# Triangular inverse of a gated delta rule: one full-array product with a crossed matrix in place of two quarter products

## The reference

```python
m = jnp.where(strict, jnp.einsum('nbhid,nbhjd->nbhij', kb, kc) * decay, 0.0)
t_inv = lax.linalg.triangular_solve(eye + m, jnp.broadcast_to(eye, m.shape), left_side=True, lower=True)
u = t_inv @ (vc * bc[..., None])
w = t_inv @ (kb * jnp.exp(gcum)[..., None])
qk = jnp.einsum('nbhid,nbhjd->nbhij', qc, kc) * decay
```

## Time and profile before

| | us |
|---|---|
| median of 3 runs | 2912.72 |
| lowest and highest of them | 2904.73, 2915.39 |
| the profiled execution | 2918.56 |
| its span on the core | 2916.8 |

### The profile page before, as it was taken

The page is one execution under the profiler, slowest core; times in us unless marked ns, Lnnn a source line. Parts: engine busy times, 40 slices in busy tenths (PEclk is TensorE's granted clock), DMA queues, the critical chain, the costliest instruction groups (busy, mean ns, idle before and its releaser), DMA issues.

```text
span 2916.8 us, 62045 instructions
## 1 busy us (share of the span) xinstructions
PE 2791.2 (96%) x24636; PEld 2709.8 (93%) x24636; DVE 2292.1 (79%) x3726; ACT 1491.2 (51%) x2527; POOL 477.1 (16%) x515
## 2 busy tenths in 40 slices
PE   5999989999999998999999999999999999999998
PEld 5999878999999998789999998899987999999998
DVE  7999766669978786666798888789877789777654
ACT  3435555554454475554545446644776544544632
POOL 0016012030110210202103011201036201102202
PEclk9999999999999999999999999999999999999999
DMA  8995403458968752135687894489421489676353
GB/s 341 349 361 204 145 17 123 141 171 327 356 221 288 246 179 82 63 113 188 249 337 260 301 327 171 147 321 344 163 95 66 159 291 345 225 270 238 130 182 136
DMA packets 173162, 632.28 MB, mean 217 GB/s; under 512 B 19216, under 2 KB 19600, under 8 KB 172560
## 3 DMA queue, kind: packets, MB, share of 16 engines
q1 hardware_dynamic: 124128, 450.82, 43.4%
q10 hardware_dynamic: 48816, 178.41, 17.3%
HBM read 628.10 MB, written 1.05 MB: 216 GB/s over the span
## 4 chain that ended last, share of the span: by engine, by line
PE 83%; DVE 10%; ACT 4%; issue 2%; DMA 1%; POOL 0%; ACTq 0%; DVEq 0%; SPq 0%
PE psum L603 24%; PE psum L605 24%; PE psum L604 24%; DVE w_lo L573 3%; DVE qkv L1433 1%; ACT w_hi L561 1%; DVE xl L2713 1%; DMA raw<-stream_dram 1%; PE psum L2811 1%; PE psum L1811 1%; PE psum L2831 1%; PE psum L2825 1%; PE psum L619 1%; ACT sm L2307 1%; PE psum L1821 0%
## 5 line engine op out<-in xcount | busy, mean ns | idle before, releaser
L603 PE MATMUL psum<-h_hi,w_hi 128*128 128x256 f32 (+1 forms) x4464 | 1268.1, 284 | 2.8 <-DVE w_lo L573 1.5
L604 PE MATMUL psum<-h_hi,w_lo 128*128 128x256 f32 (+1 forms) x4464 | 1261.2, 283 | 0.0
L605 PE MATMUL psum<-h_lo,w_hi 128*128 128x256 f32 (+1 forms) x4464 | 1259.3, 282 | 0.0
L573 DVE TENSOR_TENSOR w_lo<-raw,w_hi 128x1024 fp32r<-128x1024 f32 x852 | 1072.9, 1263 | 169.7 <-ACT w_hi L561 168.8
L561 ACT ACTIVATE w_hi<-raw 128x1024 fp32r<-128x1024 f32 x852 | 876.0, 1055 | 360.3 <-DMA raw<-stream_dram 173.2
L603 PEld LDWEIGHTS psum<-h_hi,w_hi 128*128 128x128 f32 x4464 | 850.4, 190 | 11.2 <-DVE w_lo L573 3.8
L605 PEld LDWEIGHTS psum<-h_lo,w_hi 128*128 128x128 f32 x4464 | 848.3, 190 | 0.0
L604 PEld LDWEIGHTS psum<-h_hi,w_lo 128*128 128x128 f32 x4464 | 847.4, 190 | 0.8 <-issue 0.7
L603 PE MATMUL psum<-u_hi,w_hi 128*128 128x256 f32 x1584 | 441.7, 279 | 1.3 <-ACT length L1146 1.3
L605 PE MATMUL psum<-u_lo,w_hi 128*128 128x256 f32 x1584 | 441.5, 279 | 0.0
L604 PE MATMUL psum<-u_hi,w_lo 128*128 128x256 f32 x1584 | 441.5, 279 | 0.0
(11 more groups left out here) (454 smaller groups left out, 3490.0 us busy)
## 6 DMA issues: line engine op xcount, KB each, us to landing
raw<-stream_dram SPq DMA_DIRECT2D x852, 512.0 KB, 4.1
ada_w<-ada_dram ACTq DMA_DIRECT2D x328, 512.0 KB, 5.1
tmp<-c_dram ACTq DMA_DIRECT2D x8, 512.0 KB, 4.2
x<-x_dram SPq DMA_DIRECT2D x1, 1024.0 KB, 10.0
ctx_x<-ctx_dram ACTq DMA_DIRECT2D x1, 1024.0 KB, 4.8
means<-means_dram ACTq DMA_DIRECT2D x1, 1024.0 KB, 4.8
out_dram<-tmp SPq DMA_DIRECT2D x4, 256.0 KB, 2.5
const<-const_dram SPq DMA_DIRECT2D x1, 785.0 KB, 13.5
```

The costliest lines, as they stand in the source:

```text
L573: p.nc.vector.tensor_tensor(p.w_lo[:, slot].rearrange("p k m -> p (k m)"), p.raw[:, slot], p.w_hi[:, slot].rearrange("p k m -> p (k m)").b ...
L603: mm(out, p.w_hi[:, slot, k], hi, start=start, stop=False, skip_group_check=skip)
L604: mm(out, p.w_lo[:, slot, k], hi, start=False, stop=False, skip_group_check=skip)
L605: return mm(out, p.w_hi[:, slot, k], lo, start=False, stop=stop, skip_group_check=skip)
```

## The change

Both blocks of 64 of a head and half are put into one matrix of 128x128, each in the corner off the diagonal ("crossed"), with zeros in the other two corners. One product with this matrix as the stationary operand does what two quarter products did: the upper block's result comes out in the lower partitions and the lower block's in the upper ones. Line 1811's products become half as many, each of 128 rows by 128 columns against 64 moving columns.

GpSimd makes the crossed matrix, into `decay`, by two operations per head: it copies `a_t`'s columns of block `e` to the columns of block `1 - e`, times a constant `half_e` that is one in block `e`'s partitions and zero in the others. It waits for VectorE to have written `a_t` and for ScalarE to have read `decay`. A new semaphore, `masked`, tells TensorE; only level 0 waits for it.

```diff
@@ gdn_gpsimd, for every head h
         v.tensor_tensor(p.qkv[:, h, P:T], p.qkv[:, h, P:T], p.exp_row[:, h % GROUP], ALU.mult).then_inc(p.sem["sq_done"], 1)
+        i = h % GROUP
+        pool.wait_ge(p.sem["pairs_used"], a("pairs_used") + 2 * h + 2)
+        pool.wait_ge(p.sem["turned_used"], a("turned_used") + h + 1)
+        crossed, a_t = (t.rearrange("p (c f n) -> p c f n", c=2, f=2) for t in (p.decay[:, i], p.a_t[:, i]))
+        for e in range(2):
+            ins = v.tensor_scalar(crossed[:, :, 1 - e], a_t[:, :, e], p.c(f"half_{e}"), None, ALU.mult)
+        ins.then_inc(p.sem["masked"], 1)
@@ gdn_tensor, inverse(gq), for every level and head i
                 if level:
                     pe.wait_ge(p.sem["inv_grown"], at("inv_grown", GROWN) + PAIRS + (level - 1) * GROUP + i + 1)
+                if not level:
+                    pe.wait_ge(p.sem["masked"], a("masked") + gq * GROUP + i + 1)
                 for c in range(2):
-                    for e in range(2):
-                        at_c = c * P + e * HALF
-                        ins = mm(p.psum[halves[1 - e], i, c * HALF : c * HALF + HALF],
-                                 p.a_t[halves[e], i, at_c : at_c + HALF], p.inv_h[halves[e], i, 1, c], start=True, stop=True)
+                    ins = mm(p.psum[:, i, c * HALF : c * HALF + HALF], p.decay[:, i, c * P : c * P + P],
+                             p.inv_h[:, i, 1, c], start=True, stop=True)
                 ins.then_inc(p.sem["lp_done"], 1)
```

More of the change, by code:

```diff
@@ L313, in signals @@
         n = dict(gdn_step=2 * PAIRS, cols_ready=1, exp_cum=1, rows_done=8,
-                 kb_ready=8, exponent_ready=16, row_exp=8, decay_ready=8, pairs_done=8, pairs_used=16, sq_done=8,
+                 kb_ready=8, exponent_ready=16, row_exp=8, decay_ready=8, pairs_done=8, pairs_used=16, sq_done=8, masked=8,
                  inv_grown=2 * GROWN, turned_done=8, turned_used=8, first_turned=2 * GROUP, conv_pad=1,
```

## The result

The changed kernel takes 2964.02 us (median; 2958.36 to 2973.33) against 2914.05 us of the kernel before: a ratio of 1.0163 with a 95% interval of 1.0144 to 1.0183. A second set of four executions gave 1.0169 (1.0135 to 1.0203). The profiled execution has a span of 2960.3 us in place of 2916.8, 43.5 more.

The account below looks back on a forecast made before the run. TensorE, busy 96% of the span, was taken to bound the kernel; 60.0 + 3.3 + 1.2 - 55.1 = 9.4 us more gave 2922.1 us against the median, 0.3% slower. The range ran from a little below 2909 to past 2931.5.

Parts of the forecast that it names:

- What stays. The granted clock.: Second and fourth inverse windows: the clock's fall to 1.2 GHz stays as before, costing 1.6 us each, 3.3 us together.
- Rival 3: Levels of the inverse: denser TensorE work keeps the clock up, leaving the kernel 4.5 us slower, 2917; chance 0.14.
- The price of the product: Full products in each level: 16 records at 0.110 us, paced by the weight load, 1.76 us in place of 0.94.
- the forms: Each level: switching the array from 64x64 to 128x128 and back costs 0.30 us, bounds 0.1 and 0.5.
- The stalls: Four inverse windows: all 11.3 us of "issue" waits go, as the new level needs fewer instructions per microsecond.
- Rival 1: Inverse windows: stalls are a price per instruction block, 9.4 us stay, kernel 18.8 us slower, 2931.5; chance 0.14.
- rival 2: Levels: the weight load hides behind the products, kernel 3.8 us faster, 2909; chance 0.10.
- GpSimd: Crossed matrices: 0.49 us per operation, 1.44 us per head, ready 0.4 us before TensorE needs the fourth head's.
- Rival 4: Crossed matrices: GpSimd's operations take twice as long as assumed, 7 to 11 us more, 2929 to 2933; chance 0.10.
- VectorE's slowing: First groups, ahead of the levels: busy GpSimd slows L1549 by 0.3 us and two earlier operations by 0.3; 1.2 us for both layers.
- The sum without the clock: Four inverse windows: the forecast's terms without the clock loss, 60.0 us of levels plus 1.2 for VectorE, less 55.1 before.

Follow-up runs that it names:

- the narrow train: Kernel before, TensorE idle 11.7 us, then 64 unread full-array products of 64 moving columns in the first layer (128 in the second): the 64-column train took 27.54 us.
- the kernel with the filled gap: Changed kernel plus two (second group: four) unread 256-column products where TensorE waits for VectorE ahead of the levels: 2919.11 us, 1.0021.

## Why the prediction was wrong

**The step that failed** is "What stays. The granted clock." It took two falls at 3.3 us together over from the kernel before and kept their number and their length. Neither held. The falls became three and, in the second profile, four, in the first groups too, where there had been none ahead of the merge; and each lasts 27 to 34 us where it lasted 3.4. The gap that a fall needs was there before the change, and filling it removes the fall. It is not a wait for scores, as the prediction reads it: TensorE is idle until VectorE's first steps of the inverse are done (line 1549, 1.97 us in the second groups before, 1.70 after; 0.80 and 1.08 in the first), and the change does touch it. But the length of a fall depends on the work that runs in it, which is shown, and whether it comes seems to depend on the work behind the gap, which is not. The changed levels at full clock sum to 62.17 us, and at the clock they got to 94.77: 32.6 us in the windows in place of 3.3. With the rest of the 43.5, what lies outside the windows, it is up to 36.5. Nothing else in the sum was off by more than a few microseconds. The row that should have raised doubt was the earlier trace rows: it shows a fall under work of another form, and no row showed one under narrow full products. The cost was unknown and ought to have been bounded: a clock that stays down from level 0 to the merge can at most double the 3.00 us of a level, 20 x 3.00 = 60 us more, and a rival with that price should have stood beside the others.

**Rival 3** asked about the clock too, and only in the other direction: it took denser work to be better for it. TensorE did become denser, 24.80 of 24.80 us in place of 10.4 of 14.3, and the clock stayed down all the same. The Trainium skill, "TensorE: Matmul & The Clock Gate", section "What's actually happening", has the half clock as the default that activity releases, by how busy the engine has been. By that rule, with busy read as the profile's busy time, a TensorE without gaps should have been released early in each inverse. The trace doesn't agree for the narrow product: busy for the whole of 27.54 us in the narrow train, it stayed at 1.2 GHz.

**The price of the product** was right. 16 records at 0.110 were forecast; 2.00 us from the first start to the last end, less the last one's 0.275, over 15 steps, is 0.115. The level at full clock takes 3.02 us for the forecast 3.00. What is left for the other products and the forms is 3.02 - 16 x 0.115 = 1.18, for 0.94 + 0.30. That the load sets the pace was right as well: with twice the columns moving, a level takes 3.07 us.

**The stalls** are gone as forecast: "issue" has at most 0.5% of each of the four windows, where it had 15 to 27. Rival 1, a price per block, and rival 2, a hidden load at 2.3 us a level, fall with these two.

**GpSimd** was mis-sized by a little. A crossing operation takes 0.60 us where 0.49 was assumed, and a head's turn 1.75 us (L1652 starts at 374.49 and at 376.24) in place of 1.44, so the fourth matrix was ready 0.57 us late in place of 0.4 us early:

```profile
L1658 POOL TENSOR_SCALAR decay<-a_t,const x32: 598/604/834, 371.4 to 1209.1; 128x128 f32<-128x128 f32 x32
...
374.49 0.45 POOL L1652 TENSOR_TENSOR qkv<-qkv,exp_row 128x128 f32<-128x128 f32 x1
...
376.24 0.45 POOL L1652 TENSOR_TENSOR qkv<-qkv,exp_row 128x128 f32<-128x128 f32 x1
...
378.00 1.08 PE L1818 MATMUL psum<-tmp,decay 128*128 128x64 f32 x4 [0.57 <-POOL decay L1658]
```

TensorE waits 0.57 us there. In the kernel with the filled gap it waits 0.56 in both first groups, and level 0 has 3.76 in place of 3.02 us in them. Rival 4 had the mechanism, at 7 to 11 us; it came to 2 x 0.74 = 1.5. VectorE's slowing was smaller than allowed: the gap ahead of the turns is 1.08 us where it was 0.80, 0.28 instead of 0.6 per layer. Together GpSimd costs 1.5 + 0.6 = 2.1 us for the forecast 1.2.

**The sum without the clock** would have been right to within 2 us: 62.17 - 55.12 + 0.6 = 7.7 us, where the same terms of the forecast give 60.0 + 1.2 - 55.1 = 6.1, and the filled kernel is measured at 1.0021 (1.0007 to 1.0035), that is 2 to 10 us more than before.

Still open: what decides whether a given gap brings the fall (one inverse of the changed kernel had it in one execution and not in the other), how far the narrow products behind the gap bring it about, and how many moving columns between 64 and 128 bring the clock back; it wasn't tried. No version here beats the kernel before.

## What to carry to other kernels

A product that spreads over the full array with few moving columns is a risk wherever TensorE may arrive with a low clock: ask of every stretch behind a wait not only whether the clock falls but which work will bring it back. If narrow full products can't be avoided there, fill the wait with wide products, or move the same columns twice: both cost next to nothing here and took back about 40 us. And before halving the number of products, look at what the halves shared: two quarters ran side by side, so that 32 of their records took 0.94 us, and the 16 of the full products take 16 x 0.115 = 1.84.

## What the runs showed of the hardware

- A train of full-array fp32 products with 64 moving columns, TensorE and its weight loads busy all the time, stayed at 1.2 GHz for 27.54 us; with 128 columns the clock was back within some 5 us of the start, and the train, with twice the columns, took 16.98 us. In the changed kernel the low clock lasted 27 to 34 us at a time.
- The same narrow train, begun at 2.4 GHz with no gap ahead of it, stayed there for its 14 us.
- Behind the same gap of TensorE (busy for 1.62 of 2.90 us, or 2.01 of 3.70), the clock fell in seven of eight inverses with narrow full products and in none of eight with quarter or wide ones.
- Quarter products of 64x64 with 64 columns do bring the clock back: in the kernel before 3.4 us after the fall, and with one full product in each level within the stretch from 386.5 to 390.0 us, where they had resumed at 384.35. In the changed kernel, where narrow full products have 3.67 of a level's 5.52 us, they don't.
- At full clock a full product's record takes 0.115 us with 64 columns in the mixture of a level, and the level only 0.05 us longer with 128.
- In the kernel before, a higher clock alone is worth nothing in these levels: TensorE's busy time fell by 2.4 us and "issue" took its place.
